# The recurrence's twenty feature tiles: from plain matmuls to ten units of seven block products

## What is computed

```python
h = rms_norm(x, attn_norm)
p = h @ w_in[:, recurrence]          # 2560 columns: 20 tiles of 128
prev = jnp.concatenate([p_prev[:, None], p[:, :-1]], axis=1)
xm = p + (prev - p) * mu             # mixed rows: r, k, v and the low-rank inputs
```

## Time and profile before

| | |
|---|---|
| median of 3 runs | 1608.58 us (1607.0 to 1610.33) |
| the profiled execution | 1607.88 us, of which the trace's span is 1605.9 |
| TensorE busy | 1543.2 us (96%), 13186 matmul records |
| VectorE busy | 675.7 us (42%) |
| ScalarE busy | 405.7 us (25%) |
| mean granted clock of TensorE | 0.992 of full |
| first matmul of tile 0 / of the gate columns | 25.26 / 177.31 us |
| DMA | 162.93 MB, mean 101 GB/s |

### The profile page before, as it was taken

How to read it: one execution, slowest core, us unless ns; L and a number is a source line. 1 busy time by engine, 2 the same in 40 slices (tenths; PEclk the granted TensorE clock), 3 DMA queues, 4 the chain that set the end, 5 groups by cost and what they waited for, 6 DMA issues and landing times.

```text
span 1605.9 us, 31197 instructions
## 1 busy us (share of the span) xinstructions
PE 1543.2 (96%) x13186; PEld 1200.7 (75%) x13186; DVE 675.7 (42%) x1376; ACT 405.7 (25%) x800; POOL 103.0 (6%) x186
## 2 busy tenths in 40 slices
PE   6999999999999999999999889999999999999997
PEld 4888668877777776777566766887888888888885
DVE  1112103542233225521577443222366666666663
ACT  3101135212222222411677553100121111110112
POOL 0000000011011002210400111000000000000000
PEclk9999999999999999999999999999999999999999
DMA  5222272331111125543600387332222222222221
GB/s 215 69 76 66 81 235 81 104 97 43 28 37 43 43 82 167 171 139 112 198 2 2 97 287 304 116 133 67 66 79 79 88 83 79 81 91 80 91 92 56
DMA packets 56742, 162.93 MB, mean 101 GB/s; under 512 B 7168, under 2 KB 20576, under 8 KB 55424
## 3 DMA queue, kind: packets, MB, share of 16 engines
q1 hardware_dynamic: 48032, 121.92, 24.0%
q0 software_dynamic: 7136, 35.73, 6.5%
q10 hardware_dynamic: 1440, 3.33, 0.6%
HBM read 142.96 MB, written 22.15 MB: 103 GB/s over the span
## 4 chain that ended last, share of the span: by engine, by line
PE 91%; ACT 2%; DVE 2%; issue 2%; SPq 1%; DMA 1%; ACTq 0%; DVEq 0%
PE acc L1655 22%; PE acc L960 18%; PE acc L909 9%; PE acc L1626 7%; PE acc L1684 4%; PE acc L1648 4%; PE acc L946 2%; PE acc L1055 2%; PE acc L1396 2%; PE acc L1420 2%; PE acc L934 2%; PE acc L1409 2%; PE acc L1069 1%; PE acc L1309 1%; PE acc L1027 1%
## 5 line engine op out<-in xcount | busy, mean ns | idle before, releaser
L960 PE MATMUL acc<-sb_work,sb_ring 128*128 128x272 f32 x1280 | 334.2, 404 | 1.0 <-ACT sb_work L1801 1.0
L960 PEld LDWEIGHTS acc<-sb_work,sb_ring 128*128 128x128 f32 x1280 | 231.9, 190 | 56.8 <-issue 9.9
L1655 PE MATMUL acc<-sb_work,sb_ring 128*128 128x272 f32 x856 | 207.2, 392 | 0.9 <-issue 0.9
L1655 PEld LDWEIGHTS acc<-sb_work,sb_ring 128*128 128x128 f32 x856 | 162.6, 190 | 34.7 <-issue 1.3
L909 PE MATMUL acc<-sb_work,sb_ring 128*128 128x272 f32 x640 | 148.8, 396 | 3.8 <-DVE sb_work L2136 3.8
L909 PEld LDWEIGHTS acc<-sb_work,sb_ring 128*128 128x128 f32 x640 | 122.6, 192 | 29.7 <-issue 4.2
L2085 ACT ACTIVATE sb_omemT<-acc 128x272 f32<-128x272 f32 x66 | 26.2, 396 | 349.1 <-PE acc L1655 211.1
L1655 PE MATMUL acc<-sb_work 128*128 128x272 f32 x340 | 85.1, 392 | 0.0
L2232 DVE TENSOR_TENSOR sb_work<-acc,sb_cst 128x384 f32<-128x384 f32 (+1 forms) x41 | 22.7, 553 | 127.8 <-PE acc L1055 127.8
L1655 PEld LDWEIGHTS acc<-sb_work 128*128 128x128 f32 x340 | 64.6, 190 | 13.3
L1801 ACT ACTIVATE sb_work<-acc 128x272 f32<-128x272 f32 x80 | 31.4, 394 | 162.3 <-PE acc L960 154.6
(11 more groups left out here) (414 smaller groups left out, 2340.5 us busy)
## 6 DMA issues: line engine op xcount, KB each, us to landing
sb_ring<-w_stream SPq DMA_DIRECT2D x160, 512.0 KB, 3.6
sb_work<-pages SPq DMA_DIRECT2D x64, 192.0 KB, 4.2
branch_gates<-sb_work SPq DMA_DIRECT2D x24, 272.0 KB, 4.5
sb_work<-branch_gates POOLq DMA_DIRECT2D x8, 816.0 KB, 21.4
sb_work<-mem_kT SPq DMA_DIRECT2D x8, 512.0 KB, 6.3
sb_work<-mem_v SPq DMA_DIRECT2D x8, 512.0 KB, 5.4
query_features<-sb_work SPq DMA_DIRECT2D x10, 272.0 KB, 4.3
sb_work<-x_T ACTq DMA_DIRECT2D x8, 272.0 KB, 4.8
```

What stands on the lines that cost most here:

```text
L960: mm = pe.matmul(acc[3][:, half, 0:HALF_T], fill_w[0][:, k, :], hT[:, k, half * HALF_T:(half + 1) * HALF_T], start=k == 0, stop=k == KT - 1)
L1655: mm = pe.matmul(out, w[:, q, :], x[q], start=q == 0, stop=q == n - 1)
```

## The change

Two feature tiles, c0 and c1, make a unit. Take the 8 k tiles in pairs (even, odd), the tokens in halves (LO, HI). With A0, A1 the even and odd blocks of the first tile's weights, B0, B1 those of the second, a unit is a 2 x 2 block product, formed from seven block products instead of eight (Winograd's form of Strassen's scheme), each of 4 matmuls of 272 columns:

- DVE makes from the weights s1 = B0 + B1, A0 - B0 (in place, into the ring's slot), s2 = s1 - A0 and s4 = A1 - s2, four operations of 128 x 512, once for each unit (`rw_weights`). Unit 0's stand ahead of the norm in DVE's order, the later ones inside the unit before.
- DVE makes from hT, once, three sums and one difference of 128 x 1088 each (four k pairs by 272 columns), after the whole of hT is there.
- PE runs the seven products. In unit 0 the three that need no sum of the input run side by side, pair by pair, as hT arrives.
- ACT copies two of the products out of PSUM (`rw_keep`), DVE joins the rest in seven operations of 272 columns, so that both tiles stand unscaled in SBUF, in two buffers of omemT (`raw`).
- ACT's scaling by 1 - mu and DVE's mixing then read `raw` and no longer PSUM, one unit late; the mixing's two long pieces are one of 511 columns.
- The memory tokens' sum of squares comes after unit 7, their norm in ACT after unit 8's keeps and in DVE inside unit 9. The gate columns wait for the third output of unit 9, the memory projection for its fifth.
- The FFN's semaphores are reused here, so its waits there count from higher values.

The core of the diff (declarations, most of the shifted waits of the FFN and a moved helper are left out):

```diff
+        h_sums0 = region(N_RW * T, 3, KT // 2, HALF_T)
+        h_diff0 = region(34112, KT // 2, HALF_T)
+        w_sums0 = region(scan0, 2, 3, KT // 2 * P).rearrange("p a s (q c) -> p a s q c", c=P)
+        raw = omemT[:].rearrange("p (a x) t -> p a x t", a=2)
...
+        rw_mm, rw_kept, rw_out, rw_w, rw_x = dn_mm, gu_act, gu_scaled, up_scaled, ff_done
+        N_PAIR = N_RW // 2
...
-            for n in range(N_RW):
-                w = weights(S_RW + n)
...
+            def rw_unit(u):
+                even, odd = slice(0, KT, 2), slice(1, KT, 2)
+                s1, s2, s4 = (w_sums0[:, u % 2, s] for s in range(3))
+                w = weights(S_RW + 2 * u)
+                if u == 0:
+                    weights(S_RW + 1)
+                    pe.wait_ge(rw_w, 2)
+                    for q in range(KT // 2):
+                        pe.wait_ge(hT_ready, 2 * q + 1)
+                        a = pe.matmul(bank(0, 0), w[:, 2 * q, :], hT[:, 2 * q, LO], start=q == 0, stop=q == KT // 2 - 1)
+                        pe.wait_ge(hT_ready, 2 * q + 2)
+                        b = pe.matmul(bank(0, 1), w[:, 2 * q + 1, :], hT[:, 2 * q + 1, LO], start=q == 0, stop=q == KT // 2 - 1)
+                        c = pe.matmul(bank(0, 2), s4[:, q, :], hT[:, 2 * q + 1, HI], start=q == 0, stop=q == KT // 2 - 1)
+                    for mm in (a, b, c):
+                        mm.then_inc(rw_mm, 1)
+                else:
+                    pe.wait_ge(rw_out, 5 * u - 4)
+                    run(bank(u, 0), w[:, even], [hT[:, 2 * q, LO] for q in range(KT // 2)]).then_inc(rw_mm, 1)
+                    pe.wait_ge(rw_out, 5 * u - 2)
+                    run(bank(u, 1), w[:, odd], [hT[:, 2 * q + 1, LO] for q in range(KT // 2)]).then_inc(rw_mm, 1)
+                    pe.wait_ge(rw_w, 2 * (u + 1))
+                    run(bank(u, 2), s4, [hT[:, 2 * q + 1, HI] for q in range(KT // 2)]).then_inc(rw_mm, 1)
+                w = weights(S_RW + 2 * u + 1)
+                if u == 0:
+                    pe.wait_ge(rw_x, 2)
+                else:
+                    pe.wait_ge(rw_kept, 2 * u)
+                for q in range(KT // 2):
+                    mm = pe.matmul(bank(u, 3), s2[:, q, :], h_sums0[:, 1, q], start=q == 0, stop=q == KT // 2 - 1)
+                    if q == 0:
+                        mm.then_inc(slot_used, 1)
+                mm.then_inc(rw_mm, 1)
+                if u:
+                    pe.wait_ge(rw_out, 5 * u - 1)
+                run(bank(u, 4), s1, [h_sums0[:, 0, q] for q in range(KT // 2)]).then_inc(rw_mm, 1)
+                if u == 0:
+                    pe.wait_ge(rw_x, 3)
+                else:
+                    pe.wait_ge(rw_out, 5 * u)
+                run(bank(u, 5), w[:, even], [h_diff0[:, q] for q in range(KT // 2)]).then_inc(rw_mm, 1)
+                if u == 0:
+                    pe.wait_ge(rw_x, 4)
+                pe.wait_ge(rw_kept, 2 * u + 1)
+                run(bank(u, 6), w[:, odd], [h_sums0[:, 2, q] for q in range(KT // 2)]).then_inc(slot_used, 1)
...
-            pe.wait_ge(mixed, N_RW - 1)
+            pe.wait_ge(h_rms, 2)
+            pe.wait_ge(rw_out, 5 * N_PAIR - 2)
...
+            pe.wait_ge(rw_out, 5 * N_PAIR)
...
+            def rw_keep(u, x):
+                if u >= 2:
+                    act.wait_ge(rw_out, 5 * (u - 1))
+                act.wait_ge(rw_mm, 6 * u + (1, 5)[x])
+                act.activation(kept0[:, u % 2, x], bank(u, (0, 4)[x]), ACT.Copy).then_inc(rw_kept, 1)
...
+            for u in range(N_PAIR):
+                rw_keep(u, 0)
+                if u:
+                    rw_tiles(u - 1)
+                rw_keep(u, 1)
...
+            rw_weights(0)
             dve.wait_ge(x_in[1], 16 * KT // 2)
             dve.wait_ge(h_rms, 1)
...
+            dve.wait_ge(hT_ready, KT)
+            dve.tensor_tensor(h_sums0[:, 0], hT[:, 0::2, HI], hT[:, 0::2, LO], ALU.subtract).then_inc(rw_x, 1)
+            dve.wait_ge(rw_x, 1)
+            dve.tensor_tensor(h_sums0[:, 1], hT[:, 1::2, HI], h_sums0[:, 0], ALU.subtract).then_inc(rw_x, 1)
+            dve.tensor_tensor(h_diff0, hT[:, 1::2, HI], hT[:, 0::2, HI], ALU.subtract).then_inc(rw_x, 1)
+            dve.wait_ge(rw_x, 2)
+            dve.tensor_tensor(h_sums0[:, 2], hT[:, 1::2, LO], h_sums0[:, 1], ALU.subtract).then_inc(rw_x, 1)
...
+                dve.tensor_tensor(c0[:, LO], bank(u, 1), kept0[:, u % 2, 0], ALU.add).then_inc(rw_out, 1)
+                if u + 1 < N_PAIR:
+                    rw_weights(u + 1)
...
+                    rw_mix(u - 1)
+                dve.wait_ge(rw_mm, 6 * u + 4)
+                dve.tensor_tensor(shared0, bank(u, 3), kept0[:, u % 2, 0], ALU.add).then_inc(rw_out, 1)
+                dve.wait_ge(rw_out, 5 * u + 2)
+                dve.tensor_tensor(c0[:, HI], bank(u, 2), shared0, ALU.add).then_inc(rw_out, 1)
+                dve.wait_ge(rw_mm, 6 * u + 6)
+                dve.tensor_tensor(shared0, bank(u, 5), shared0, ALU.add).then_inc(rw_out, 1)
+                dve.wait_ge(rw_kept, 2 * u + 2)
+                dve.wait_ge(rw_out, 5 * u + 4)
+                own(dve.tensor_tensor(c0[:, HI], c0[:, HI], kept0[:, u % 2, 1], ALU.add))
+                own(dve.tensor_tensor(c1[:, HI], shared0, kept0[:, u % 2, 1], ALU.add))
...
+                dve.wait_ge(slot_used, S_RW + 2 * u + 2)
+                dve.tensor_tensor(c1[:, LO], bank(u, 6), shared0, ALU.add).then_inc(rw_out, 1)
```

More of the change, by code:

```diff
@@ L897, in _, with run @@
                 mm.then_inc(h_sum, 1)
-            for n in range(N_RW):
-                w = weights(S_RW + n)
[L901 to L913, removed]
+            def run(out, w, x):
+                n = len(x)
+                for q in range(n):
+                    mm = pe.matmul(out, w[:, q, :], x[q], start=q == 0, stop=q == n - 1)
+                return mm
@@ L1650, in _ @@
                 mm.then_inc(slot_used, 1)
[L1652 to L1656, removed]
             def unit(u, x, x0, sums, diffs):
@@ L2131, in _, with rw_weights @@
             dve.tensor_scalar(ka1, v("ka", 0, PAIRS), -1.0, 1.0, ALU.mult, ALU.add).then_inc(means, 1)
+            def rw_weights(u):
+                slots = [S_RW + 2 * u + x for x in range(2)]
+                a, b = (ring[:, n % RING, :].rearrange("p (k c) -> p k c", c=P) for n in slots)
+                s1, s2, s4 = (w_sums0[:, u % 2, s] for s in range(3))
+                for n in slots:
+                    dve.wait_ge(w_in_slot[n % RING], 16 * (n // RING + 1))
+                if u >= 2:
+                    dve.wait_ge(slot_used, S_RW + 2 * (u - 1))
+                own(dve.tensor_tensor(s1, b[:, 0::2], b[:, 1::2], ALU.add))
+                dve.tensor_tensor(b[:, 0::2], a[:, 0::2], b[:, 0::2], ALU.subtract).then_inc(rw_w, 1)
+                own(dve.tensor_tensor(s2, s1, a[:, 0::2], ALU.subtract))
+                dve.tensor_tensor(s4, a[:, 1::2], s2, ALU.subtract).then_inc(rw_w, 1)
+            rw_weights(0)
             dve.wait_ge(x_in[1], 16 * KT // 2)
@@ new lines, in rw_mix @@
+            def rw_mix(u):
+                for e in range(2):
+                    n = 2 * u + e
+                    x, y, mu = rwT[:, n, :], raw[:, u % 2, e, :], v("mu", n)
+                    dve.wait_ge(rw_evicted, n + 1)
+                    dve.tensor_copy(shift_now[:, n, :], y[:, TP - 1:T:NQ])
+                    dve.scalar_tensor_tensor(x[:, 1:TP], y[:, 0:TP - 1], mu, x[:, 1:TP], ALU.mult, ALU.add)
+                    xs, ys = (a[:, TP:T].rearrange("p (b q) -> p b q", q=NQ) for a in (x, y))
+                    dve.scalar_tensor_tensor(xs[:, :, 1:], ys[:, :, 0:NQ - 1], mu, xs[:, :, 1:], ALU.mult, ALU.add)\
+                       .then_inc(mixed, 1)
@@ new lines, in _ @@
+            for u in range(N_PAIR):
+                c0, c1 = raw[:, u % 2, 0, :], raw[:, u % 2, 1, :]
+                if u:
+                    dve.wait_ge(rw_out, 5 * u)
+                dve.wait_ge(rw_kept, 2 * u + 1)
+                dve.wait_ge(rw_mm, 6 * u + 2)
+                dve.tensor_tensor(c0[:, LO], bank(u, 1), kept0[:, u % 2, 0], ALU.add).then_inc(rw_out, 1)
+                if u + 1 < N_PAIR:
+                    rw_weights(u + 1)
+                if u == 0:
+                    dve.wait_ge(rw_in, 48)
+                    own(dve.tensor_tensor(shift9, shift9, bc(v("mu", 0, N_RW), 2, NB), ALU.mult))
+                else:
+                    rw_mix(u - 1)
[9 more added lines that the diff above has]
+                own(dve.tensor_tensor(c1[:, HI], shared0, kept0[:, u % 2, 1], ALU.add))
+                if u == N_PAIR - 1:
```

57 lines of the change are left out of this document (27 added, 30 removed).

## The result

The changed kernel's median is **1594.19 us** (five runs, 1591.51 to 1602.69), that of the kernel before, run beside it, 1607.02 (five runs, 1605.18 to 1610.33); the ratio is 0.9933 with a 95% interval of 0.9908 to 0.9958. The forecast was 1590.5, range 1586.5 to 1594.5: the right sign, the median just inside the range, but only 10.8 us gained by the ratio where 18.1 were forecast (12.8 by these medians). The profiled execution is the slowest of the five, 1602.69 us, with a span of 1600.8; against 1605.9 it shows only 5.1 us. That makes it a good witness of where a gain can go.

The account below looks back on a forecast made before the run. TensorE was taken to bound the stage, so fewer matmuls meant less time: 16.5 us from nine steady units plus 1.6 from unit 0, 18.1 us, gave 1589.8 profiled and a median of 1590.5 us, range 1586.5 to 1594.5.

Parts of the forecast that it names:

- Part 1: Recurrence, steady units 1 to 9: 12.83 us each instead of 14.67 for two tiles, saving 16.5 us together.
- VectorE's share: Steady unit: VectorE's weight sums, joins and mixing were to take 8.2 us of the 12.83.
- the ring: Weight load slots in steady units: two loads per 12.83 us, one issued 10 us before use; cost nothing.
- rivals of the joins: Steady units: VectorE's queue of joins, sums and mixing becomes the bound, 15.5 us a unit, 1614.5 us; chance 0.03.
- bank waits: Steady units: matmuls fall but waits for banks fill the 1.83 us saved, time within 3.2 us of 1608.6; chance 0.02.
- Part 2: Unit 0 and the start: ends at 40.2 us, 1.6 us before tiles 0 and 1 did.
- the wide sums: Unit 0: VectorE's input sums of 1088 columns at 1.27 us each; at 1.77 TensorE would wait 0.7.
- The late load: Start: second weight load lands at 24.3 us, norm begins at 27.1, everything 2.7 later, 1593.2 us; chance 0.08.
- Part 3: End of the recurrence: memory sum keeps 3.45 us; gate columns, 7.45 us, cover the memory norm with 4 us to spare.
- All later stages are chained to PE's or POOL's own events and should move as a block: After the recurrence: the whole saving carries through, gates starting at 159.2 us instead of 177.31.
- The rival of the clock: Half-clock stretches: one more or fewer later, 3.4 us either way, or longer at unit 0, 1.7; chance 0.14 for both.
- The prediction's own test: Sign of being wrong: gates near 159 us but span not 18 us shorter, putting the loss downstream.

Follow-up runs that it names:

- equal places: Kernel before and changed kernel compared with TensorE filling chosen so that later instructions lie alike in the 256-instruction code pieces; changed with 156 against plain before: ratio 0.9901.
- the changed kernel at the places of before: Changed kernel plus 156 filling instructions ahead of TensorE's first matmul, restoring later code places: 1604.18 us with semaphore increments, 1589.92 us with tiny matmuls.
- the trace of 76: Changed kernel plus 19 tiny matmuls (76 filling instructions) in TensorE's idle start: 1588.48 us, again 1588.09 us.
- 156 and 332 of filling: Changed kernel plus 156 or 332 filling instructions ahead of TensorE's first matmul: 1604.18 us (156 increments), 1589.92 us (156, tiny matmuls), 1588.36 us (332, tiny matmuls).
- the form in turn: Changed kernel with 76 filling instructions, but unit 0's first three products one after another instead of side by side: 1591.57 and 1588.83 us.

## Why the prediction was right, and where it was wrong

- **Part 1, nine units of 12.83 us:** right, to the hundredth. VectorE's share was 0.8 us too high. ACT, the ring and the banks cost nothing, as said; the rivals of the joins and of the bank waits did not occur.
- **Part 2, unit 0:** right. 8.45 us for 8.57, the wide sums 1.29 for 1.27; TensorE's weight loads stood 0.3 us for them before 31.69, its matmuls lost some 0.1. The late load cost 0.4 us, not 2.7.
- **Part 3, the end of the stage:** right; the gates keep their 7.46 us and the memory norm was covered.
- **The step that failed** is "All later stages are chained to PE's or POOL's own events and should move as a block". What waits for what did not change, but TensorE's code is itself a supply, and the change moved where it is cut. The program is 156 instructions shorter ahead of the gates. At its own places TensorE pauses 6 to 9 us from 318 to 622 us, where before it paused 2, and behind some of the pauses the clock is low for 3.4 us. Of 18 us 5 to 8 went so in the medians of the three sets of runs of the plain changed kernel (12.8, 10.5 and 9.8 us remained), 13 in the profiled execution. At equal places the forecast holds within some 2.5 us (15.9 to 20.6 for 18.1), and the block does move as one: from the gates to the end it is 1428.6 us before and 1428.4 and 1429.9 in the changed kernel at the places of before, and in the trace of 76 it is 20.6 us early at 219 and 20.9 at the end (2.65 of it from an earlier norm). That the plain changed kernel's median still fell inside the range, by 0.3 us, is luck: the range was drawn for the clock and the start, not for this.
- **The rival of the clock** got the right symptom for another reason: more low stretches, but behind new pauses and not because a stretch began at another time. Its size, 3.4 either way, was too small: from 200 to 1500 us the low stretches sum to 30.7 us, where they summed to 17.1, which is 6.8 at half price. At unit 0 the low stretch lasted 3.4 us in the changed kernel's three traces, as before; with 156 and 332 of filling it lasted 6.8, and the gates came 0.5 us later after the norm, not 1.7. The prediction's own test, "a gates start near 159 and yet a span not 18 us shorter", is what came.
- The Trainium skill (Runtime: NRT & Kernel Launch, Instruction fetch mechanics) says that code is refilled in 16 KiB blocks of 256 instructions and that the cost of crossing one is "mostly hidden". The runs agree on the size: the pauses lie whole multiples of 256 instructions apart. On the cost they agree for some cuts only: 2.1 to 3.7 us of pauses in some 300 us against 4.5 to 9.1.

**Open.** Why one cut is hidden and the next is not isn't settled: only the modulus and the small matmuls around it are shown. From 860 to 1010 us the pauses put down to issue are 7.2 us before, 8.6 after, and 2.7 to 11.4 in the experiments; their places follow the cuts there too, but their lengths differ at equal places (8.9, 6.2 and 2.7 with 76, 76 and 332). From the gates to the end the profiled execution of the changed kernel lost 14.0 us: all pauses at cuts from 330 to 1560 us are 8.1 more than before, and the low stretches 6.8. The same sum comes 4 us short for the second trace of 76, so a part remains unexplained. How much the clock adds by itself was not tried alone. In one trace of the form in turn the pauses are 2.8 us, but the low stretches from 200 to 1500 us sum to 23.9, and gates to end took 1433.6 us, so that some microseconds come and go without the pauses.

## What to carry to other kernels

Count the instructions that an edit adds to or removes from an engine's straight code, not only their time: in stages of small matmuls a cut of the code in another place was worth as much as half of this change. When a gain that is plain in its own stage is missing at the end, compare the same instruction in both traces along the span, and look for pauses put down to "issue" where it drifts. Then try a few amounts of filling in an idle place before you judge the edit, and compare kernels at equal places.

## What was not expected of the hardware

- TensorE paused up to 2.5 us from 318 to 622 us, and up to 3.4 behind 860, in code for which the trace shows no branch of TensorE. In 139 of the 140 pauses it resumed 1.0 to 1.6 us after a packet of code had ended.
- Pauses as short as 1.2 to 1.7 us were followed some 0.3 to 0.6 us later by 3.4 us at 1.2 GHz, three times in the profiled execution, though TensorE was busy before and after. It is not so each time: the longest pause, 2.20, had no such stretch behind it, nor had the one of 1.17 with 76.
- 156 semaphore increments in a row took 154 ns each on TensorE; tiny fp32 matmuls (128 rows, 4 x 4 out) took 1.09 us for 38 matmul records, 29 ns each, in a time that was idle.
- The norm's start, which waits for the first loads, was at 23.24, 22.14 and 22.43 us in three executions of the same program; that is part of the spread inside every kernel's runs.
